# By-token products in 512-column tiles, ordered by token tile around each norm, in a two-block transformer kernel

## The reference

```python
# block 1, each of 2 layers            (x is 256 x 1024)
h   = x @ w_in                                   # 1024 -> 1704 columns: q, k, v, index heads
mix = concat(window_attn, sparse_attn) @ w_o     # 1024 -> 1024
x   = layer_norm(ALPHA * x + mix)
ffn = (silu(x @ w_gate) * (x @ w_up)) @ w_down   # 1024 -> 2816 -> 1024
ple = (p @ w_pp) * sigmoid(x @ w_pg)
x   = layer_norm(ALPHA * x + ffn + ple)
# block 2, each of 2 layers            (first: x = layer_norm(x) once more)
h   = x @ w_in_2                                 # 1024 -> 1976 columns
x   = layer_norm(ALPHA * x + concat(mla, nsa) @ w_out)
x   = layer_norm(ALPHA * x + cross_attention(x, memory) @ xa_wo)
x   = layer_norm(ALPHA * x + conv_ffn(x))
```

## Time and profile before

| | |
|---|---|
| median of 3 runs | 1730.0 us |
| the profiled execution | 1732.68 us |
| its span, first to last instruction | 1730.8 us |
| mean granted TensorE clock | 0.948 of full speed |
| PE busy / weight loads / DVE / ACT / POOL | 91% / 86% / 63% / 43% / 4% |
| instructions | 27619, of which 11573 matmuls |

### The profile page before, as it was taken

How to read it: one execution, slowest core, us unless ns; L and a number is a source line. 1 busy time by engine, 2 the same in 40 slices (tenths; PEclk the granted TensorE clock), 3 DMA queues, 4 the chain that set the end, 5 groups by cost and what they waited for, 6 DMA issues and landing times.

```text
span 1730.8 us, 27619 instructions
## 1 busy us (share of the span) xinstructions
PE 1578.7 (91%) x11573; PEld 1492.9 (86%) x11573; DVE 1095.0 (63%) x1710; ACT 750.9 (43%) x1060; POOL 62.8 (4%) x58
## 2 busy tenths in 40 slices
PE   6889899999888999968988989999899899999997
PEld 6889899998778999958878888999798788889996
DVE  6975855557866855465545647767755546477666
ACT  4554333334562433323656334545436553344442
POOL 0200000000100000010000000000010000000000
PEclk8989999999899999988989999999988899999998
DMA  9423555555323565553513624555535145245551
GB/s 304 154 82 108 177 177 188 194 174 179 114 92 122 196 218 185 181 170 94 170 59 101 207 88 153 202 191 189 176 96 185 46 141 188 90 171 180 193 185 59
DMA packets 215424, 267.48 MB, mean 155 GB/s; under 512 B 7382, under 2 KB 196740, under 8 KB 215172
## 3 DMA queue, kind: packets, MB, share of 16 engines
q1 hardware_dynamic: 210404, 260.48, 45.5%
q10 hardware_dynamic: 4896, 5.25, 0.9%
HBM read 260.46 MB, written 5.24 MB: 154 GB/s over the span
## 4 chain that ended last, share of the span: by engine, by line
PE 76%; DVE 12%; DVEq 3%; ACT 3%; issue 3%; POOL 2%; DMA 0%; SPq 0%; POOLq 0%; ACTq 0%
PE psw L587 17%; PE psw L588 17%; PE psw L589 17%; PE psa L587 5%; PE psa L588 5%; PE psa L589 5%; DVE wlo L1335 3%; PE psa L723 2%; POOL rstd L1934 2%; PE psw L706 1%; DVE sy L1408 1%; DVE xtok L1363 1%; PE psw L1043 1%; ACT whi L1062 1%; PE psw L1025 1%
## 5 line engine op out<-in xcount | busy, mean ns | idle before, releaser
L1335 DVE TENSOR_TENSOR wlo<-raw,whi 128x2048 fp32r<-128x2048 f32 (+1 forms) x230 | 520.2, 2265 | 327.8 <-ACT whi L1062 327.3
L1062 ACT ACTIVATE whi<-raw 128x2048 fp32r<-128x2048 f32 (+1 forms) x230 | 434.6, 1890 | 363.3 <-PE psw L589 261.1
L587 PE MATMUL psw<-xhi,whi 128*128 128x256 f32 x1536 | 438.4, 285 | 3.0 <-DVE xlo L1375 1.6
L588 PE MATMUL psw<-xlo,whi 128*128 128x256 f32 x1536 | 437.7, 285 | 0.0
L589 PE MATMUL psw<-xhi,wlo 128*128 128x256 f32 x1536 | 437.5, 285 | 0.0
L587 PEld LDWEIGHTS psw<-xhi,whi 128*128 128x128 f32 x1536 | 298.1, 194 | 5.9 <-issue 2.8
L588 PEld LDWEIGHTS psw<-xlo,whi 128*128 128x128 f32 x1536 | 298.1, 194 | 1.2
L589 PEld LDWEIGHTS psw<-xhi,wlo 128*128 128x128 f32 x1536 | 297.9, 194 | 0.0
L587 PE MATMUL psw<-whi,xhi 128*128 128x256 f32 (+2 forms) x992 | 288.2, 291 | 8.0 <-DVE xlo L1375 8.0
L588 PE MATMUL psw<-wlo,xhi 128*128 128x256 f32 (+2 forms) x992 | 286.0, 288 | 0.0
L589 PE MATMUL psw<-whi,xlo 128*128 128x256 f32 (+2 forms) x992 | 285.8, 288 | 0.0
(11 more groups left out here) (257 smaller groups left out, 2001.9 us busy)
## 6 DMA issues: line engine op xcount, KB each, us to landing
raw<-in_w_gu SPq DMA_DIRECT2D x44, 1024.0 KB, 5.1
raw<-in_ffn_w_up SPq DMA_DIRECT2D x44, 1024.0 KB, 5.1
raw<-in_w_in SPq DMA_DIRECT2D x26, 1024.0 KB, 5.3
raw<-in_w_down SPq DMA_DIRECT2D x22, 1024.0 KB, 4.9
raw<-in_ffn_w_down SPq DMA_DIRECT2D x22, 1024.0 KB, 4.8
raw<-in_xa_wkv SPq DMA_DIRECT2D x16, 1024.0 KB, 5.3
raw<-in_w_o SPq DMA_DIRECT2D x8, 1024.0 KB, 5.0
raw<-in_w_pg SPq DMA_DIRECT2D x8, 1024.0 KB, 4.9
```

The costliest lines, as they stand in the source:

```text
L587: pe.matmul(o, lh, rh, start=first, stop=False)
L588: pe.matmul(o, lh, rl, start=False, stop=False)
L1062: nc.scalar.activation(tile_flat(whi, NW, i), tile_flat(raw, NL, i), ACT.Copy).then_inc(hi_ready, 1)
L1335: v.tensor_tensor(tile_flat(wlo, NL, i), tile_flat(raw, NL, i), tile_flat(whi, NW, i).bitcast(F32), ALU.subtract).then_inc(lo_ready, 1)
```

## The change

1. Tiles. in1, o, pg, in2, out and xo are cut in groups of 512 columns, each in two pieces of four feature tiles (`by_groups`); in1 has groups of 424, 512, 512 and 256 columns, in2 of 512, 512, 512 and 440. The number of tiles and the bytes stay the same, the product pp of block 1 is made in 512 columns too.
2. Order. `token_stage` runs over pieces q and token tiles t in the order of `passes(n, head, tail)`: the first `head` pieces for tile 0, then for tile 1, the middle ones for both in turn, the last `tail` ones again by token tile. in1, in2 and pg have head 3; o, out and xo have tail 3. The norm's turns of tile 0 stand ahead of the last piece for tile 1; those of tile 1 stand behind two pieces for tile 0 of the next stage, or directly behind the stage where xq or the FFN follows. The last two down tiles are interleaved by token tile and half.
3. Turned activations lie in banks by token tile (always in `psa`), so that `xhi` and `xlo` of tile 0 can be made alone; `norm`, `turned_hi` and `turned_lo` take one token tile.
4. One extra weight tile buffer (`ext`, and `sy[:, 1]` as its raw buffer), used by the first tile of pg, xq, the FFN behind xo, in1 of layer 1 and in2. `plan_extra` names the tile whose end frees it.

```diff
+def plan_extra(ti):
+    extra = {}
+    for l in range(L):
+        extra[ti[(1, "pg", l, 0)]] = ti[(1, "o", l, 0)]
+        extra[ti[(2, "xq", l, 0)]] = ti[(2, "out", l, 0)]
+        extra[ti[(2, "g", l, 0)]] = ti[(2, "xo", l, 0)]
+    extra[ti[(1, "in", 1, 0)]] = ti[(1, "pg", 0, 0)]
+    extra[ti[(2, "in", 0, 0)]] = ti[(1, "pg", 1, 0)]
+    extra[ti[(2, "in", 1, 0)]] = ti[(2, "g", 0, 0)]
+    return extra
+def passes(n, head, tail):
+    both = [(q, t) for q in range(head, n - tail) for t in range(NT)]
+    return ([(q, t) for t in range(NT) for q in range(head)] + both +
+            [(q, t) for t in range(NT) for q in range(n - tail, n)])
+    def room(i, n):
+        if i in extra:
+            return extra[i] + 1
+        return ring[seq[i] - n] + 1 if seq[i] >= n else 0
...
# SP
-                if i >= NL:
-                    sp.wait_ge(tile_done, i - NL + 1)
+                if room(i, NL):
+                    sp.wait_ge(tile_done, room(i, NL))
...
# PE
+                token_stage(1, "in", l, 7, x_in, 3, 0, bank_free,
+                            {(2, 0): lambda: norm_turns(x_in, 1), (3, 0): memory_turns, (5, 0): first_heads,
+                             (6, 0): first_scores})
...
+                token_stage(1, "o", l, 4, (1, "mix", l), 0, 3, before={(3, 1): lambda: norm_turns((1, "1", l), 0)})
+                token_stage(1, "pg", l, 4, (1, "1", l), 3, 0, before={(2, 0): lambda: norm_turns((1, "1", l), 1)})
...
+                token_stage(2, "out", l, 4, (2, "mix", l), 0, 3, before={(3, 1): lambda: norm_turns((2, "1", l), 0)})
+                norm_turns((2, "1", l), 1)
...
+                for t in range(NT):
+                    for half in range(2):
+                        ins = down(FS - 2, t, half)
+                        if t == 1 and half == 1:
+                            ins.then_inc(tile_done, 1)
+                        ins = down(FS - 1, t, half)
+                        ins.then_inc(tile_done if t == 1 and half == 1 else part_done, 1)
...
# ACT and DVE
             def serve(key):
-                while nxt[0] <= min(ti[key] + NW, n_tiles - 1):
+                while nxt[0] < n_tiles and room(nxt[0], NW) <= ti[key] + 1:
...
# DVE, around o, out and xo
+                serve((block, name, l, 0))
+                for half in range(2):
+                    dve.wait_ge(part_done, part[(block, name, l, half)])
+                    join(0, half)
+                norm(norm_key, xtok, 0)
+                serve((block, name, l, 1))
+                turned_lo(norm_key, 0)
+                for half in range(2):
+                    dve.wait_ge(tile_done, ti[(block, name, l, 2 * half + 1)] + 1)
+                    join(1, half)
+                norm(norm_key, xtok, 1)
+                if by_features:
+                    turned_lo(norm_key, 1)
+                serve((block, name, l, 2))
+                if not by_features:
+                    turned_lo(norm_key, 1)
+                serve((block, name, l, 3))
...
# DVE, at the end of an FFN
+                joined(0, 0)
+                joined(0, 1)
+                norms_of(0)
+                joined(1, 0)
+                if early:
+                    turned_lo(turn_key, 0)
+                joined(1, 1)
+                norms_of(1)
+                if turn_key is not None:
+                    if not early:
+                        turned_lo(turn_key, 0)
+                    serve((block, "d", l, FS - 2))
+                    serve(key)
+                    turned_lo(turn_key, 1)
...
# DVE, start of in1
                 if l == 0:
+                    turned_lo((1, "in", 0), 0)
                     split(2)
                     nxt[0] = 3
+                    turned_lo((1, "in", 0), 1)
                     angles()
                 serve((1, "pp", l, 0))
```

More of the change, by code:

```diff
@@ L95, in plan_tiles, with by_groups @@
     tiles = []
+    geo = {}
     def rows(a):
         return a.rearrange("(k p) n -> p k n", p=P)
+    def by_groups(block, name, l, a, groups):
+        q = 0
+        for g, (c0, c1) in enumerate(groups):
+            pieces = 2 if c1 - c0 > TC else 1
+            kt = KD // pieces
+            for piece in range(pieces):
+                key = (block, name, l, q)
+                tiles.append((key, a[:, piece * kt:(piece + 1) * kt, c0:c1]))
+                geo[key] = (g, piece * kt, piece == pieces - 1)
+                q += 1
+    halves = ((0, 512), (512, 1024))
     def ffn(block, l, gate, up, down):
@@ L118, in plan_tiles @@
         tiles.append(((1, "pp", l, 0), rows(w["w_pp"][l])))
[L119 to L120 removed]
+        by_groups(1, "in", l, rows(w["w_in"][l]), IN1_GROUPS)
         memory_tiles(1, l)
[L122 to L125, removed]
+        by_groups(1, "o", l, rows(w["w_o"][l]), halves)
+        by_groups(1, "pg", l, rows(w["w_pg"][l]), halves)
         gu = rows(w["w_gu"][l])
@@ L128, in plan_tiles @@
     for l in range(L):
-        for k in range(8):
-            tiles.append(((2, "in", l, k), rows(w["w_in_2"][l])[:, :, k * TC:min((k + 1) * TC, IN2)]))
+        by_groups(2, "in", l, rows(w["w_in_2"][l]), IN2_GROUPS)
         for k in range(2):
@@ L161, in build @@
 def build(nc, w, c, out):
-    tiles, ti = plan_tiles(w)
+    tiles, ti, geo = plan_tiles(w)
+    extra = plan_extra(ti)
+    ring = [i for i in range(len(tiles)) if i not in extra]
+    seq = {i: q for q, i in enumerate(ring)}
+    extra_use = {i: e for e, i in enumerate(sorted(extra))}
     units, chunk0 = plan_units()
     n_tiles = len(tiles)
+    def room(i, n):
+        if i in extra:
+            return extra[i] + 1
+        return ring[seq[i] - n] + 1 if seq[i] >= n else 0
     slots = {1: SLOTS1, 2: SLOTS2}
@@ L429, in add_norm @@
         def add_norm(key, g, b, place=gb):
-            norms[key] = dict(n=len(norms), g=g, b=b, place=place, loads=sum("g" in x for x in norms.values()) + 1)
+            norms[key] = dict(n=len(norms) - (block_two in norms), g=g, b=b, place=place,
+                              loads=sum("g" in x for x in norms.values()) + 1)
+        block_two = (2, "in", 0)
         add_norm((1, "in", 0), w["ln_in_g"], w["ln_in_b"])
@@ L602, in by_tokens @@
                 ins.then_inc(tile_done, 1)
[L604 to L623, removed]
             def by_features(key, bank, ah, al, ready=None):
@@ L1429, in attention @@
                         serve((2, "kv", half // 16, half // 2 % 8))
-            def residual_norm(keys, norm_key):
-                def piece(k, ts, ps):
-                    cols = slice(k * TC, (k + 1) * TC)
-                    ins = v.scalar_tensor_tensor(out=xtok[:, ts, cols], in0=xtok[:, ts, cols], scalar=ALPHA,
-                                                 in1=ps, op0=ALU.mult, op1=ALU.add)
-                    if k < 2:
-                        ins.then_inc(joined, 1)
-                    dve.drain()
-                    for t in range(ts.start, ts.stop):
-                        v.bn_stats(stats[:, t, k, :], xtok[:, t, cols])
-                for k in range(2):
-                    dve.wait_ge(tile_done, ti[keys[k]] + 1)
-                    piece(k, slice(0, NT), bank2(psw, k))
-                    serve(keys[k])
-                def last(t):
-                    for k in (2, 3):
-                        if t == 0:
-                            dve.wait_ge(part_done, part[keys[3]])
-                        else:
-                            dve.wait_ge(tile_done, ti[keys[k]] + 1)
-                        piece(k, slice(t, t + 1), residual_banks(k)[t].unsqueeze(1))
-                norm(norm_key, xtok, 4, last)
@@ L1458, in ffn_norm, with joined @@
+            def ffn_norm(block, l, norm_key, join, next_key=None, turn_key=None, early=True):
                 key = (block, "d", l, FS - 1)
-                def last(t):
-                    if t == 0:
-                        dve.wait_ge(part_done, part[key])
-                    else:
-                        dve.wait_ge(tile_done, ti[key] + 1)
-                    for half in range(2):
-                        join(t, slice(half * 512, (half + 1) * 512), psa[:, 2 * t + half, :])
+                def joined(t, half):
+                    h = slice(half * 512, (half + 1) * 512)
+                    if t and half:
+                        dve.wait_ge(tile_done, ti[key] + 1)
+                    else:
+                        dve.wait_ge(part_done, part[(block, "d", l, 2 * t + half)])
+                    join(t, h, psa[:, 2 * t + half, :])
@@ L1467, in last, with norms_of @@
                     dve.drain()
-                    half_stats(xtok, t)
-                for t in range(NT):
-                    norm(norm_key, xtok, 2, last, [t])
+                    v.bn_stats(stats[:, t, half, :], xtok[:, t, h])
+                def norms_of(t):
+                    norm(norm_key, xtok, t, next_key is None)
                     if next_key is not None:
-                        norm(next_key, xtok, 2, lambda t: (dve.drain(), half_stats(xtok, t)), [t])
+                        dve.drain()
```

(2 more changed lines are left out.)

590 lines of the change are left out of this document (334 added, 256 removed).

## The result

The changed kernel takes 1743.5 us (median of 4 runs, 1741.6 to 1747.4) beside 1729.8 (4 runs) for the kernel before on the same chip: ratio 1.0073, 95% interval 1.0060 to 1.0086. It is slower by 13 us; the forecast was 1724, with a range of 1704 to 1742. The profiled execution took 1741.6, 8.9 more than the one of before; it lies 1.9 under its median where the other lay 2.8 over.

The account below looks back on a forecast made before the run. The prediction took PE, busy for 91% of the span, as the bound. Its gains and losses summed to +6.3 us, taking the profiled 1732.7 to 1726.4 and the median to 1723.7, forecast as 1724, range 1704 to 1742.

Parts of the forecast that it names:

- Ends of block 2's FFNs: Block 2, last down tiles: layer 0 to 1 gains 5.3 us, the tail after the last layer gains 1.2.
- PE stops for 2.1, new: Block 2, last down tiles: PE waits 2.1 us for the last hidden tile, a wait not there before.
- At nothing: Attention, gate, up and the FFN's steady part keep their order, so they change by 0.
- Out and xo: Block 2's boundaries: out to xq loses 12.7 us for both layers, xo to the FFN loses 6.1.
- o: Block 1, o through pg to the FFN: 51.05 us against 56.25 and 55.44 before, a gain of 9.6.
- Width: Projections: one 512-column product replacing two of 256 saves 0.0128 us; in2's two layers gain 7.0 us.
- Start: Layer 0 of in1: a delayed third piece and weight split are passed on, a loss of 14 us (11 to 17).
- three signs of being wrong: Out to xq under 30 us, in 3's split before 42, or a mean clock under 0.93.
- A: Rival: out and xo start the next stage as early as before, 18.8 us less, 1705; chance 0.20.
- D: Rival: the start is cheap because DVE catches up in in1, 1710; chance 0.12.
- C: Rival: 512 columns stream no faster per column than two of 256, 19 us lost, 1743; chance 0.04.
- B: Rival: about ten short new PE waits each lower the clock, 17 us lost, about 1740; chance 0.22.

Follow-up runs that it names:

- e6: Changed kernel with the extra tile split behind the last hidden tile in each FFN's last step: ratio 1.0047 to the kernel before, 4.5 us less than the changed kernel.
- e7: Changed kernel with the last but one down tile's products issued first for both halves of a token tile: ratio 1.0003 to the kernel before, 12.1 us less.
- e2: Changed kernel with keys' and values' loads behind the second xq tile and norm parameters loaded earlier: ratio 1.0021 to the kernel before, 9.0 us less.
- e3: Changed kernel with DVE's splits (and ACT's copies) put behind the norms around o, out and xo: ratio 0.9994 to the kernel before, 13.7 us less.
- e10: Changed kernel with the first tiles of xq and block 2's FFN back in the buffer ring: ratio 0.9960 to the kernel before, 19.6 us less.
- e1: Changed kernel with two head pieces instead of three in layer 0 of in1: ratio 1.0000 to the kernel before, 12.6 us less than the changed kernel.
- e4: Changed kernel with by-token products wider than 256 columns issued as two, order kept: ratio 1.0142 to the kernel before, 12.0 us more than the changed kernel.
- e8: Changed kernel with 20 unread products in PE's wait ahead of tile 1's turns in out and xo: ratio 1.0020 to the kernel before, 9.2 us less.

## Why the prediction was wrong

The mechanisms were right, and their sum had the wrong sign: +6.3 foretold, -8.9 measured in the profiled executions. The table gives the 15.2 between them, term by term:

- *Ends of block 2's FFNs, 6.5 of it* ("+5.3" with its in2, and "+1.2" for the tail). The step that failed is "PE stops for 2.1, new". The wait of 2.1 was there (1.95 in layer 1), but in layer 0 the extra tile's split stood ahead of the hidden tile and made it 4.15 (e6), and both waits were followed by products at a granted clock of 0.80 and 0.85 (e7). The prediction wrote that in block 1 the last hidden tile "is there in time"; PE waited 1.82 there for the same split, hidden in that span's other waits (the span came within 0.3).
- *"At nothing", 4.5*: the four FFNs took 3.0 longer. In block 1 their first tile waits 0.75 and 0.48 for `wlo`, behind the splits that now queue up in pg; this was not tried by itself. The 1.5 in the attention is no more than its scatter.
- *Out and xo, 3.6*, sized -18.8 and measured -22.4. The order of events was right; e2, e3 and e10 confirm SP's hold and DVE's split as their causes. At 12.7 for out it was short by 2.8, most of it in layer 1.
- *o, 1.9*: 51.76 and 52.28 for 51.05. In each layer one piece behind a set of turns ran in part at half the clock, which the sum took at full: 12 products in 4.05 for 2.73 behind tile 0's turns in layer 0, and in 4.37 behind tile 1's in layer 1.
- *Width* was sized right: 512 columns at 0.2267 (foretold 0.2272), 424 at 0.193 (0.191), 440 at 0.202 (0.197).
- *Start*: -12.3 and -0.7 for -14, 1.0 better; block 1's boundaries and in1 are within 0.4 of their sizes, and xq to xo was 0.7 better than nothing.
- *The scale*: the profiled execution of before lay 2.8 above its median and the one of after 1.9 below its own. That is 4.6 of the 19.8 between 1723.7 and 1743.5.

None of the three signs of being wrong that the prediction named came up (out to xq 36.74 and 38.04, in 3's split at 50.20, a mean clock of 0.944): they watched the mechanisms, and not the small margin that decided.

The rivals. A (boundaries free) fell with the windows out to xq. D fell with e1. C fell with e4. B forecast 1740, near the result, by a mechanism that only e7 and e8 show at work: the clock behind the new waits cost some 4.3 at the FFNs' ends and 4.1 at their starts, of which the kernel before paid 3.1 too (171.87 and 172.19 against 170.46). So B is worth about 5 of the 17 it was given. A second estimate gives 8: with every distance between two product starts that has no wait in it set against the same width's distance at full clock, the kernel before loses 29.6 us to the lower clock and the changed one 37.2, and 5.2 of the 7.6 between them lie behind S' of block 2's FFNs. The loss is that of the start and of the extra tile: undone alone, each is worth about as much as the whole slowdown or more (12.6 and 19.6 for 13).

The prediction had these two losses in its sum, at 32.8 together, and came out faster because the gains were credited in full: its margin of 6.3 stood on a dozen terms that were each uncertain by 1 to 5. A chance of 0.60 for faster was too much for that.

## What to carry to other kernels

A tile prefetched into an extra buffer isn't free on engines that work in order: its load and its split take a place ahead of something. Here that was a norm or the last hidden tile, and it cost its own length, PE's wait and the clock behind it (19.6 us around the norms by e10_no_extra, 4.5 at the hidden tile by e6_hold_extra). Place the split behind the critical step, or leave the tile in the ring, before you add a buffer. And if a sum of large terms leaves a small margin, say first which of them can be removed by itself: here two single edits turned +0.73% into nothing and into -0.4%, and four of them with the filling behind xo into -1.9%.

## What was not expected of the hardware

Work that nobody reads can pay. 20 products in a wait of 5.7 us took the granted clock of the next 48 from 0.74 and 0.67 to 1.00 and saved 1.7 and 2.4 us there. And the length of the wait doesn't settle it: behind 1.95 us of waiting in the last down tiles the clock was 0.85, behind 2.79 in e7's it was 1.00. Which of the two a wait brings was not found out.
